# Low halves of the merge-gate weights: a subtraction on VectorE, or an adding transfer onto a negated high half

## The chip, the core and the metric

One core of a Trainium2 chip runs the whole kernel. The metric is device time in microseconds from one launch, the median of several executions. TensorE multiplies, VectorE and ScalarE work elementwise, GpSimd and SyncE here only issue transfers, and sixteen DMA engines carry them.

## What is computed

The reference is a trunk of two layers on 512 tokens of width 1024 (float32). In each layer the normalized input is multiplied by a wide matrix `w_in`; three mixers (sliding-window attention with sinks, gated linear attention, latent attention) work on its parts; and three gates of 1024 channels each weigh their projected outputs:

```python
(qa, ka, va, ga, qb, kb, vb, ab, gb, cq, ckv, kr, gc, mg) = split_cols(h @ w_in)
...
m = jax.nn.sigmoid(mg).reshape(B, S, N_BRANCH, D_MODEL)
y = m[:, :, 0] * za + m[:, :, 1] * zb + m[:, :, 2] * zc
return x + y @ w_out
```

The columns `mg` of `w_in`, 3072 of them, are the merge-gate weights that the change is about.

## The kernel before

**Pieces.** All weights lie in memory as 77 pieces for each layer, 128 partitions by 1024 float32 (512 KB), in the order of their use. `pieces[n]` with n = 77 x layer + p is loaded into `raw`, which has three slots. Every product is made of three matmuls in a reduced-width float type: with a weight split into a high half and a low half, and the input split likewise, it is high x high, high x low and low x high. The halves of a piece lie in `w_hi` and `w_lo`, which have three slots each (`HL = RAW = 3`), n modulo 3. Most pieces hold 128 output columns for a depth of 1024, so they take 8 x 3 = 24 matmuls of 128x128 by 512.

**Who does what to a piece n.**
- SyncE (line 563) waits until the subtraction of piece n - 3 is done (`lo_split`), then issues the load of piece n (line 564). The same queue issues, between these loads, 12 of every 16 transfers that place turned tiles of attention scores (`place_blocks`, line 495), 0.6 us each, so a load waits its turn behind them.
- ScalarE (`split_hi`, line 903) waits for the load and until TensorE has finished piece n - 3, then copies `raw` to `w_hi` with a cast (line 909). It also computes the tanh of each gate (line 1055), the exponentials of the attention scores (lines 1117 and 1129), and issues the other 4 of each 16 transfers.
- VectorE (`split_lo`, line 1208) waits for that copy and subtracts: `w_lo = raw - w_hi` (line 1215). It also empties the accumulation banks (line 1545), makes the silu gates (line 1419), divides and transposes the scores (lines 1485, 1498, 1514) and gates the branches' outputs (line 1230).
- TensorE (`project`, line 577) waits for the subtraction of piece p at its first quarter (line 583) and then issues its matmuls (line 657).
- GpSimd has no work.

**The order.** Each engine walks the same hand-written list, `SCHEDULE`, made by `make_schedule`: quarters of pieces, with named steps between them ("score_a", "divide_a", "turn_a", "send", "value_c", "gate_c" and so on). An engine acts on the names that concern it, strictly in this order. At the second quarter of piece p VectorE splits piece p + 2; at the last quarter ScalarE splits piece p + 3, then does the tanh of piece p, then the steps that follow. So what comes late on an engine makes everything behind it in the list late on that engine.

**The merge-gate pieces** are 22 to 29, 38 to 45 and 57 to 64 of each layer (`PM = [22, 38, 57]`, eight from each), 48 in all. During the first run the linear attention's output is normalized and turned; in the second the sliding-window scores are exponentiated, divided, turned and used (lines 1117, 1485, 1514, 735, 1230); ahead of and in the third run it is the latent attention's scores (lines 868, 1129, 1498, 892). A turned tile leaves VectorE's transposes, is placed by 16 transfers, and is read by the value matmuls (lines 735, 892), which write a bank that VectorE's gate (line 1230) empties.

Of the kernel before, what the change touches and what calls it, by code (L numbers as in the profile page):

```python
# [19 lines left out]
ALU = mybir.AluOpType  # L20
ACT = mybir.ActivationFunctionType
AX_X = mybir.AxisListType.X

DEPTH, D, S, CHUNK, P = 2, 1024, 512, 64, 128
# [20 lines left out]
PM = [22, 38, 57]  # L45
PO = [30, 49, 65]
PUKV, PUQ = 46, 47
PW = 69
PIECES = 77
RAW = HL = 3  # L50
# [33 lines left out]
def emptied_by(r):  # L84

    by_scalar = by_act(r + 1) > by_act(r)
    return not by_scalar, by_scalar


def signals_before(p):  # L90

    return sum(max(outputs_of(q), 1) for q in range(p))
# [212 lines left out]
def build_hybrid_trunk(nc, x_t, pieces, params, alpha, tables, consts, final_g, out, k_rope_dram):  # L305
    with ExitStack() as ctx:
# [3 lines left out]
        def sig(name, per_layer, before=0):  # L310
            return Signal(ctx, nc, name, per_layer, before)
# [5 lines left out]
        raw = sb("raw", [P, RAW, 1024])  # L317
        w_hi = sb("w_hi", [P, HL, 1024], F32R)
        w_lo = sb("w_lo", [P, HL, 1024], F32R)
# [99 lines left out]
        head_hi, head_lo = sig("head_hi", 0), sig("head_lo", 0)  # L419
        eps_set, ones_set = sig("eps_set", 0), sig("ones_set", 0)  # L420
        lat_sq_hi, lat_sq_lo = sig("lat_sq_hi", 2), sig("lat_sq_lo", 2)
        hi_split, lo_split = sig("hi_split", PIECES), sig("lo_split", PIECES)
        proj_done = sig("proj_done", signals_before(PIECES), HL + 1)
        proj_free = sig("proj_free", by_dve(first_output(PIECES)), KT)
        ring_act = sig("ring_act", by_act(first_output(PIECES)))
# [62 lines left out]
        block = ctx.enter_context(nc.Block())  # L488
# [10 lines left out]
        def _(sp):  # L499
            for j in range(KT):  # L500
                sp.dma_start(xt[:, j, :], x_t[:, j, :]).then_inc(x_loaded[j].sem, 16)
                if j == 2:
                    for n in range(2, 4):
                        p, cols = HEADS[n]
# [9 lines left out]
            for n in range(RAW + 1, DEPTH * PIECES):  # L514
                layer, p = divmod(n - RAW, PIECES)
                if p in (PQA[1] + 3, PQA[3] + 3):

                    pair = (PQA[1] + 3, PQA[3] + 3).index(p)
                    sp.wait_ge(rope_out.sem, rope_out.at(layer, 6 + 2 * pair))
                    for hh in range(GROUP):  # L520
                        for half in range(2):
                            sp.dma_start(q_a[64 * pair + 32 * half:64 * pair + 32 * half + 32, hh, :],
                                         work[32 * hh:32 * hh + 32, 4 + half, :]).then_inc(q_placed.sem, 16)
                elif p == PUKV + 3:

                    sp.wait_ge(k_rope_saved.sem, k_rope_saved.at(layer, 16))
                    sp.wait_ge(read_done.sem, read_done.at(layer, 4))
                    for a in range(GROUP):
                        sp.dma_start(k_r[32 * a:32 * a + 32, :], k_rope_dram).then_inc(k_rope_placed.sem, 16)
                elif p == PUQ + 4:  # L530

                    sp.wait_ge(rope_out.sem, rope_out.at(layer, 10))
                    for g, half, a in ((g, half, a) for g in range(2) for half in range(2) for a in range(GROUP)):
                        sp.dma_start(q_r[32 * a + 16 * half:32 * a + 16 * half + 16, g, :],
                                     work[64 * g + 16 * a:64 * g + 16 * a + 16, 2 * half, :]).then_inc(q_rope_placed.sem, 16)
                if p == PM[0] + 3:

                    sp.wait_ge(head_blocks.sem, head_blocks.at(layer, 4))
                    sp.wait_ge(read_done.sem, read_done.at(layer, 4))
                    for n_part in range(SP_PARTS):  # L540
                        place_blocks(sp, 0, n_part, head_placed)
                for group in SENDS.get(p, ()):

                    sp.wait_ge(blocks_set.sem, blocks_set.at(layer, 4 * group + 4))
                    if group < 2:
                        sp.wait_ge(y_pre_set.sem, y_pre_set.at(layer, B_HEADS))
                    elif group > 2:
                        sp.wait_ge(value_done.sem, value_done.at(layer, TT + group - 3))
                    for n_part in range(SP_PARTS):
                        place_blocks(sp, group, n_part, turned_placed)  # L550
                if layer == DEPTH - 1 and PW <= p < PW + 4:

                    m = p - PW
                    sp.wait_ge(x_turned.sem, KT)
                    sp.wait_ge(value_done.sem, value_done.at(layer, TT + n_sets))
                    for b in range(4):
                        sp.dma_start(x_rows[32 * m:32 * m + 32, :, 256 * b:256 * b + 256],
                                     bank_a[32 * b:32 * b + 32, 1024 * m:1024 * m + 1024].rearrange("p (t d) -> p t d", t=TT)
                                     ).then_inc(rows_placed.sem, 16)
                if layer == DEPTH - 1 and p == PW + 4:  # L560
                    sp.wait_ge(merge_lo.sem, merge_lo.at(layer, KT))
                    sp.dma_start(gain, final_g).then_inc(gain_loaded.sem, 16)
                sp.wait_ge(lo_split.sem, n - RAW + 1)
                sp.dma_start(raw[:, n % RAW, :], pieces[n]).then_inc(raw_loaded[n % RAW].sem, 16)
            for t in range(TT):
                sp.wait_ge(scaled_dve.sem, t + 1)
# [9 lines left out]
        def _(pe):  # L576
            def project(layer, quarter):

                p, part = divmod(quarter, 4)
                slot = (layer * PIECES + p) % HL  # L580
                whi, wlo = w_hi[:, slot, :], w_lo[:, slot, :]
                if part == 0:
                    pe.wait_ge(lo_split.sem, lo_split.at(layer, p + 1))
                natural = p in PN1 or p in PN2
                n_out = outputs_of(p)

# [76 lines left out]
            def last_rows():  # L663

                layer, banks = DEPTH - 1, [*(r[:, :] for r in ring), aux[:, :]]

                def row_tile(p, k, t, bank):

                    slot, ts = (layer * PIECES + p) % HL, slice(t * P, (t + 1) * P)
                    cols = slice(k % 2 * HALF, k % 2 * HALF + HALF)  # L670
                    pe.matmul(bank, act_hi[:, k, ts], w_hi[:, slot, cols], start=k == 0, stop=False)  # L671
                    pe.matmul(bank, act_lo[:, k, ts], w_hi[:, slot, cols], start=False, stop=False)  # L672
                    return pe.matmul(bank, act_hi[:, k, ts], w_lo[:, slot, cols], start=False, stop=k == KT - 1)  # L673

                for n in range(4):
                    pe.wait_ge(lo_split.sem, lo_split.at(layer, PW + n + 1))
                    for k in (2 * n, 2 * n + 1):
                        pe.wait_ge(merge_lo.sem, merge_lo.at(layer, k + 1))
                        for t in range(TT):
                            mm = row_tile(PW + n, k, t, nat[t])  # L680
                    mm.then_inc(proj_done.sem, 1)
                pe.wait_ge(proj_free.sem, proj_free.at(layer, by_dve(first_output(PW))))
                pe.wait_ge(o_read.sem, o_read.at(layer, 2 * TT))
                for n in range(2):
                    pe.wait_ge(lo_split.sem, lo_split.at(layer, PW + 4 + n + 1))
                    for k in (2 * n, 2 * n + 1):
                        for t in range(TT):
                            mm = row_tile(PW + 4 + n, k, t, banks[t])
                    mm.then_inc(proj_done.sem, 1)
                for t in range(TT):  # L690
                    for n in range(2, 4):
                        if t == 0:
                            pe.wait_ge(lo_split.sem, lo_split.at(layer, PW + 4 + n + 1))
                        for k in (2 * n, 2 * n + 1):
                            mm = row_tile(PW + 4 + n, k, t, banks[t])
                    mm.then_inc(rows_done.sem, 1)
# [52 lines left out]
            for layer in range(DEPTH):  # L749
                u = 0  # L750
                for name, i in SCHEDULE:
# [82 lines left out]
                    elif name == "score_a":  # L834

                        ready, n = (head_nat, 4) if i == 0 else (exp_done, 4)
# [65 lines left out]
        def _(act):  # L902
            def split_hi(layer, p):

                n = layer * PIECES + p
                act.wait_ge(raw_loaded[n % RAW].sem, 16 * (n // RAW + 1))

                act.wait_ge(proj_done.sem, proj_done.at(layer, signals_before(p - HL + 1) if p >= HL else p - HL + 1))
                nc.scalar.activation(w_hi[:, n % HL, :], raw[:, n % RAW, :], ACT.Copy).then_inc(hi_split.sem, 1)  # L909

            def rms_of(layer, u, place, dst, n, tmp):
# [266 lines left out]
            act.dma_start(out[TT - 1, :, 0:HALF], out_first[:, TT - 1, :]).then_inc(out_sent[1].sem, 16)  # L1178


        @block.vector
        def _(dve):
            def add_square(layer, n):
# [24 lines left out]
            def split_lo(layer, p):  # L1208

                if p >= PIECES:  # L1210
                    layer, p = layer + 1, p - PIECES
                if layer < DEPTH:
                    dve.wait_ge(hi_split.sem, hi_split.at(layer, p + 1))
                    n = layer * PIECES + p
                    nc.vector.tensor_tensor(w_lo[:, n % HL, :], raw[:, n % RAW, :], w_hi[:, n % HL, :].bitcast(F32),  # L1215
                                            ALU.subtract).then_inc(lo_split.sem, 1)
# [555 lines left out]
```

## Time and profile before

| what | us |
|---|---|
| median of three executions (931.48 to 931.8) | 931.62 |
| span of the profiled execution, first to last instruction | 929.7 |
| TensorE busy | 922.0 |
| VectorE busy | 601.2 |
| ScalarE busy | 387.2 |
| GpSimd busy | 0.2 |

The time of the profiled execution is given by its span; the median of the timed ones is 1.9 us longer. A row of a timeline gives the start, the length, engine, line, operation, output and inputs, and in brackets how long the engine had been idle before and what ended that. ACT is ScalarE, DVE VectorE, PE TensorE, SPq and ACTq the transfers that SyncE and ScalarE issue. Matmuls overlap: a row of 0.39 us is followed by the next 0.23 us after its start.

### The profile page before, as it was taken

What the parts mean: (1) busy time and instruction counts of PE and PEld (TensorE: products, weight loads), DVE (VectorE), ACT (ScalarE), POOL (GpSimd) and SP (SyncE); (2) the same over time, 40 slices, a digit from 0 to 9 for tenths busy, and PEclk for the clock granted to TensorE, in tenths of its full rate; (3) what the DMA queues carried; (4) which work ended last, traced back from release to release, by engine and by line L of the source; (5) the groups of instructions that cost most, each with busy time, mean ns of one, the idle gap of its engine ahead of it and who ended that gap; (6) DMA issues with size and microseconds to landing.
All of it is one profiled execution on the core that took longest, in us unless ns stands there. A gap on an engine that the chain in (4) does not pass through costs nothing.

```text
span 929.7 us, 13082 instructions
## 1 busy us (share of the span) xinstructions
PE 922.0 (99%) x5108; PEld 755.8 (81%) x5108; DVE 601.2 (65%) x982; ACT 387.2 (42%) x724; POOL 0.2 (0%) x4
## 2 busy tenths in 40 slices
PE   9999999999999999999999999999999999999997
PEld 7988888888888777888889888888888887778886
DVE  7856467448757877575457664674477568876834
ACT  7453344324543454432444333442264425562324
POOL 0000000000000000000000000000000000000000
PEclk9999999999999999999999999999999999999999
DMA  7324324322434255422232333253234433454542
GB/s 292 136 70 147 114 69 136 113 91 80 140 122 140 85 151 150 145 92 90 91 113 91 95 108 106 68 163 109 91 92 143 140 114 109 122 156 136 146 127 90
DMA packets 43789, 110.98 MB, mean 119 GB/s; under 512 B 8592, under 2 KB 11408, under 8 KB 43600
## 3 DMA queue, kind: packets, MB, share of 16 engines
q1 hardware_dynamic: 39664, 104.82, 35.8%
q10 hardware_dynamic: 4064, 5.33, 2.2%
q8 instruction: 40, 0.66, 0.3%
q14 instruction: 21, 0.17, 0.1%
HBM read 85.41 MB, written 2.23 MB: 94 GB/s over the span
## 4 chain that ended last, share of the span: by engine, by line
PE 86%; DVE 5%; ACT 3%; SPq 2%; issue 1%; DMA 1%; ACTq 1%; DVEq 0%
PE ring L657 65%; PE nat L657 9%; PE nat L868 3%; PE aux L892 2%; SPq L495 1%; DVE w_lo L1215 1%; ACT work L1117 1%; PE nat L672 1%; PE nat L671 1%; PE nat L673 1%; DVE work L1514 1%; DMA raw<-pieces 1%; ACT w_hi L909 1%; PE ring L672 1%; PE ring L671 1%
## 5 line engine op out<-in xcount | busy, mean ns | idle before, releaser
L657 PE MATMUL ring<-act_hi,w_hi 128*128 128x512 f32 x784 | 308.7, 394 | 0.0
L657 PE MATMUL ring<-act_lo,w_hi 128*128 128x512 f32 x784 | 305.5, 390 | 0.0
L657 PE MATMUL ring<-act_hi,w_lo 128*128 128x512 f32 x784 | 305.2, 389 | 0.0
L909 ACT ACTIVATE w_hi<-raw 128x1024 fp32r<-128x1024 f32 x152 | 161.7, 1064 | 340.5 <-PE ring L657 275.5
L1215 DVE TENSOR_TENSOR w_lo<-raw,w_hi 128x1024 fp32r<-128x1024 f32 x152 | 184.6, 1216 | 82.7 <-ACT w_hi L909 82.3
L657 PEld LDWEIGHTS ring<-act_hi,w_hi 128*128 128x128 f32 x784 | 147.1, 188 | 38.2 <-issue 8.4
L657 PEld LDWEIGHTS ring<-act_hi,w_lo 128*128 128x128 f32 x784 | 147.2, 188 | 31.1
L657 PEld LDWEIGHTS ring<-act_lo,w_hi 128*128 128x128 f32 x784 | 147.2, 188 | 29.7
L1545 DVE SCALAR_TENSOR_TENSOR gates<-ring,rstd 128x512 f32<-128x512 f32 x72 | 49.3, 685 | 77.0 <-PE ring L657 76.8
L657 PE MATMUL ring<-y_hi,w_hi 128*128 128x512 f32 x192 | 74.9, 390 | 0.0
L657 PE MATMUL ring<-y_hi,w_lo 128*128 128x512 f32 x192 | 74.7, 389 | 0.0
L657 PE MATMUL ring<-y_lo,w_hi 128*128 128x512 f32 x192 | 74.7, 389 | 0.0
L1055 ACT ACTIVATE gates<-gates 128x512 f32<-128x512 f32 x72 | 45.1, 626 | 18.9 <-DVE gates L1545 18.9
L657 PE MATMUL nat<-w_hi,act_hi 128*128 128x512 f32 (+1 forms) x128 | 48.1, 376 | 0.3 <-DVE w_lo L1215 0.3
L657 PE MATMUL nat<-w_lo,act_hi 128*128 128x512 f32 (+1 forms) x128 | 47.8, 374 | 0.0
L657 PE MATMUL nat<-w_hi,act_lo 128*128 128x512 f32 (+1 forms) x128 | 47.8, 374 | 0.0
L1129 ACT ACTIVATE work<-nat,neg_top 128x256 f32<-128x256 f32 (+3 forms) x48 | 24.7, 530 | 43.9 <-DVE neg_top L1472 43.9
L657 PEld LDWEIGHTS ring<-y_hi,w_hi 128*128 128x128 f32 x192 | 36.0, 188 | 8.1 <-issue 0.7
L657 PEld LDWEIGHTS ring<-y_hi,w_lo 128*128 128x128 f32 x192 | 36.0, 188 | 7.5
L657 PEld LDWEIGHTS ring<-y_lo,w_hi 128*128 128x128 f32 x192 | 36.1, 188 | 7.4
L1595 DVE SCALAR_TENSOR_TENSOR gates<-gates,ring 128x512 f32<-128x512 f32 x32 | 21.9, 685 | 9.0 <-PE ring L657 8.9
L657 PEld LDWEIGHTS nat<-w_hi,act_hi 128*128 128x128 f32 x128 | 24.1, 188 | 3.9 <-DVE w_lo L1215 0.8
(227 smaller groups left out, 995.6 us busy)
## 6 DMA issues: line engine op xcount, KB each, us to landing
raw<-pieces SPq DMA_DIRECT2D x152, 512.0 KB, 3.5
bank_g<-work SPq DMA_DIRECT2D x120, 64.0 KB, 2.0
lat<-work SPq DMA_DIRECT2D x72, 64.0 KB, 2.0
bank_g<-work ACTq DMA_DIRECT2D x40, 64.0 KB, 2.2
xt<-x_t SPq DMA_DIRECT2D x8, 256.0 KB, 4.9
bank_a<-work SPq DMA_DIRECT2D x32, 64.0 KB, 2.0
bank_g<-bank_a SPq DMA_DIRECT2D x16, 128.0 KB, 3.9
out<-gates SPq DMA_DIRECT2D x7, 256.0 KB, 2.1
```

The lines of the kernel that those rows point to most:

```text
L495: engine.dma_start(dst[32 * j:32 * j + 32, S * i:S * i + S], work[32 * i:32 * i + 32, 3 + j, :]).then_inc(placed.sem, 16)
L657: mm = pe.matmul(dst, stationary, moving, start=start and i == 0, stop=stop and i == 2)
L671: pe.matmul(bank, act_hi[:, k, ts], w_hi[:, slot, cols], start=k == 0, stop=False)
L672: pe.matmul(bank, act_lo[:, k, ts], w_hi[:, slot, cols], start=False, stop=False)
L868: mm = pe.matmul(nat[a][:, col:col + n], q, k, start=part == 0, stop=part == 2)
L892: mm = pe.matmul(o_t[r * 64:r * 64 + 64, place, :].rearrange("p (i n) -> p i n", i=4), v_c[:, b, h * C_V:(h + 1) * C_V], turned_c[2 - i % ...
L909: nc.scalar.activation(w_hi[:, n % HL, :], raw[:, n % RAW, :], ACT.Copy).then_inc(hi_split.sem, 1)
L1055: nc.scalar.activation(gates[:, j if j >= 4 else 8 + j, :], gates[:, j, :], ACT.Tanh).then_inc(gate_tanh.sem, 1)
L1129: one = nc.scalar.activation(prob[a][:, keys], nat[a][:, keys], ACT.Exp, scale=C_SCALE, bias=neg_top[:, i % 2, 4 * n + a:4 * n + a + 1], a ...
L1215: nc.vector.tensor_tensor(w_lo[:, n % HL, :], raw[:, n % RAW, :], w_hi[:, n % HL, :].bitcast(F32), ALU.subtract).then_inc(lo_split.sem, 1)
L1545: nc.vector.scalar_tensor_tensor(gates[:, j, :], res, 0.5, rstd[:, :], ALU.mult, ALU.mult).then_inc(proj_free.sem, 1)
L1595: nc.vector.scalar_tensor_tensor(merged[:, j, :] if b == 0 else tile, tile, 1.0, z, ALU.add, ALU.mult).then_inc(proj_free.sem, 1)
```

## The change

For the 48 merge-gate pieces ScalarE writes two tiles from `raw`: first minus the high half into `w_lo`, then the high half into `w_hi`. GpSimd waits for the first, and issues a transfer that reads the piece from memory once more and adds it onto `w_lo`, which then holds the low half. VectorE's subtraction of these pieces is gone. TensorE waits for the landing and for the copy to `w_hi`; there is one semaphore for landings in each slot. SyncE frees a slot of `raw` when both of ScalarE's tiles are written. All other pieces stay as they are, with the counts of `lo_split` taken over them alone.

```diff
+LO_BY_DMA = {p for first in PM for p in range(first, first + 8)}
+
+def lo_by_dve(n):
+    return sum(m % PIECES not in LO_BY_DMA for m in range(n))
+
+def lo_by_dma(n, slot=None):
+    return sum(m % PIECES in LO_BY_DMA and slot in (None, m % HL) for m in range(n))
...
-                sp.wait_ge(lo_split.sem, n - RAW + 1)
+                if p in LO_BY_DMA:
+                    sp.wait_ge(neg_set.sem, lo_by_dma(n - RAW + 1))
+                    sp.wait_ge(hi_split.sem, n - RAW + 1)
+                else:
+                    sp.wait_ge(lo_split.sem, lo_by_dve(n - RAW + 1))
                 sp.dma_start(raw[:, n % RAW, :], pieces[n]).then_inc(raw_loaded[n % RAW].sem, 16)
...
-                    pe.wait_ge(lo_split.sem, lo_split.at(layer, p + 1))
+                    n = layer * PIECES + p
+                    if p in LO_BY_DMA:
+                        pe.wait_ge(lo_added[slot].sem, 16 * lo_by_dma(n + 1, slot))
+                        pe.wait_ge(hi_split.sem, hi_split.at(layer, p + 1))
+                    else:
+                        pe.wait_ge(lo_split.sem, lo_by_dve(n + 1))
...
+                if p in LO_BY_DMA:
+                    nc.scalar.activation(w_lo[:, n % HL, :], raw[:, n % RAW, :], ACT.Copy, scale=-1.0).then_inc(neg_set.sem, 1)
                 nc.scalar.activation(w_hi[:, n % HL, :], raw[:, n % RAW, :], ACT.Copy).then_inc(hi_split.sem, 1)
...
+        @block.gpsimd
+        def _(pool):
+            for n in range(DEPTH * PIECES):
+                if n % PIECES in LO_BY_DMA:
+                    pool.wait_ge(neg_set.sem, lo_by_dma(n + 1))
+                    pool.dma_start(w_lo[:, n % HL, :], pieces[n], accum_op=ALU.add).then_inc(lo_added[n % HL].sem, 16)
...
-                if layer < DEPTH:
+                if layer < DEPTH and p not in LO_BY_DMA:
                     dve.wait_ge(hi_split.sem, hi_split.at(layer, p + 1))
```

## Rows read from the trace of the kernel before

**Rows 1.** The page, part 1: busy us, share, instructions.
```profile
PE 922.0 (99%) x5108; PEld 755.8 (81%) x5108; DVE 601.2 (65%) x982; ACT 387.2 (42%) x724; POOL 0.2 (0%) x4
```

**Rows 2.** The chain of waits, whole run: start us, us, what.
```profile
126.84 84.59 PE ring L657 x372
```

**Rows 3.** Waits of TensorE, whole run: us in total, times, longest us.
```profile
PE aux L744 <- DVE merged L1232: 1.2, 1, 1.2
PE aux L735 <- DMA bank_g<-work: 0.4, 2, 0.2
PE nat L657 <- DVE w_lo L1215: 0.3, 1, 0.3
```

**Rows 4.** The page, part 5: copies to w_hi and subtractions to w_lo.
```profile
L909 ACT ACTIVATE w_hi<-raw 128x1024 fp32r<-128x1024 f32 x152 | 161.7, 1064 | 340.5 <-PE ring L657 275.5
L1215 DVE TENSOR_TENSOR w_lo<-raw,w_hi 128x1024 fp32r<-128x1024 f32 x152 | 184.6, 1216 | 82.7 <-ACT w_hi L909 82.3
```

**Rows 5.** Timeline of ScalarE, 224 to 246 us.
```profile
224.57 1.06 ACT L909 ACTIVATE w_hi<-raw 128x1024 fp32r<-128x1024 f32 x1 [2.18 <-PE ring L657]
225.54 0.62 ACT L1055 ACTIVATE gates<-gates 128x512 f32<-128x512 f32 x1
230.15 2.72 ACTq L495 DMA_DIRECT2D bank_g<-work  x4
232.97 0.21 ACT L1112 ACTIVATE sink_exp<-top 128x8 f32<-128x8 f32 x1 [6.81 <-DVE top L1454]
...
238.68 1.14 ACT L909 ACTIVATE w_hi<-raw 128x1024 fp32r<-128x1024 f32 x1
...
243.07 1.06 ACT L909 ACTIVATE w_hi<-raw 128x1024 fp32r<-128x1024 f32 x1 [0.73 <-PE ring L657]
```

**Rows 6.** Timeline of ScalarE, 129 to 131 us: start, us, what [idle before].
```profile
129.92 1.06 ACT L909 ACTIVATE w_hi<-raw 128x1024 fp32r<-128x1024 f32 x1 [0.95 <-PE ring L657]
```

**Rows 7.** Transfers: queue of SyncE, loads of raw, their landing over the run.
```profile
q1 hardware_dynamic: 39664, 104.82, 35.8%
...
raw<-pieces SPq DMA_DIRECT2D x152, 512.0 KB, 3.5
...
DMA to landing us min/median/max: 3.3/3.5/7.2
```

**Rows 8.** Timeline of SyncE's transfers, 237 to 248 us.
```profile
237.68 9.90 SPq L564 DMA_DIRECT2D raw<-pieces  x4
```

**Rows 9.** Timelines of ScalarE and VectorE, 144 to 151 us.
```profile
149.60 1.06 ACT L909 ACTIVATE w_hi<-raw 128x1024 fp32r<-128x1024 f32 x1 [2.07 <-issue]
...
144.48 1.18 DVE L1215 TENSOR_TENSOR w_lo<-raw,w_hi 128x1024 fp32r<-128x1024 f32 x1
145.59 0.68 DVE L1419 SCALAR_TENSOR_TENSOR gates<-gates 128x512 f32<-128x512 f32 x1
```

**Rows 10.** Timeline of VectorE, 226 to 231 us.
```profile
226.19 0.69 DVE L1419 SCALAR_TENSOR_TENSOR gates<-gates 128x512 f32<-128x512 f32 x1 [0.28 <-ACT gates L1055]
...
230.04 1.18 DVE L1215 TENSOR_TENSOR w_lo<-raw,w_hi 128x1024 fp32r<-128x1024 f32 x1
```

**Rows 11.** Timeline of ScalarE, second layer, copy of piece 41.
```profile
697.04 1.15 ACT L909 ACTIVATE w_hi<-raw 128x1024 fp32r<-128x1024 f32 x1
```

**Rows 12.** Timelines of ScalarE, VectorE and TensorE, 343 to 350 us.
```profile
343.40 1.10 ACT L909 ACTIVATE w_hi<-raw 128x1024 fp32r<-128x1024 f32 x1
344.92 0.63 ACT L1055 ACTIVATE gates<-gates 128x512 f32<-128x512 f32 x1 [0.42 <-DVE gates L1545]
...
344.81 1.47 DVE L1419 SCALAR_TENSOR_TENSOR gates<-gates 128x512 f32<-128x512 f32 x2
...
348.06 0.39 PE L657 MATMUL ring<-act_hi,w_lo 128*128 128x512 f32 x1
348.50 0.77 PE L892 MATMUL aux<-bank_g,bank_a 128*64 128x128 f32 x10
```

More of the change, by code:

```diff
@@ L421, in build_hybrid_trunk @@
         lat_sq_hi, lat_sq_lo = sig("lat_sq_hi", 2), sig("lat_sq_lo", 2)
-        hi_split, lo_split = sig("hi_split", PIECES), sig("lo_split", PIECES)
+        hi_split, lo_split = sig("hi_split", PIECES), sig("lo_split", lo_by_dve(PIECES))
+        neg_set, lo_added = sig("neg_set", 0), [sig(f"lo_added{i}", 0) for i in range(HL)]
         proj_done = sig("proj_done", signals_before(PIECES), HL + 1)
@@ L675, in last_rows @@
                 for n in range(4):
-                    pe.wait_ge(lo_split.sem, lo_split.at(layer, PW + n + 1))
+                    pe.wait_ge(lo_split.sem, lo_by_dve(layer * PIECES + PW + n + 1))
                     for k in (2 * n, 2 * n + 1):
@@ L684, in last_rows @@
                 for n in range(2):
-                    pe.wait_ge(lo_split.sem, lo_split.at(layer, PW + 4 + n + 1))
+                    pe.wait_ge(lo_split.sem, lo_by_dve(layer * PIECES + PW + 4 + n + 1))
                     for k in (2 * n, 2 * n + 1):
@@ L692, in last_rows @@
                         if t == 0:
-                            pe.wait_ge(lo_split.sem, lo_split.at(layer, PW + 4 + n + 1))
+                            pe.wait_ge(lo_split.sem, lo_by_dve(layer * PIECES + PW + 4 + n + 1))
                         for k in (2 * n, 2 * n + 1):
```

## Prediction

> **What bounds the kernel now.** I read the page's busy shares first: TensorE is busy for 922.0 of 929.7 us while VectorE works 601.2 us [rows 1]. A busy TensorE need not be a full one, so the next view is the chain of waits: one link is 372 matmuls in 84.59 us [rows 2], which is 0.2274 us for each, with nothing between them. A piece of 24 matmuls so lasts 5.46 us, and in that stretch the vector engines set nothing. The third view, TensorE's own waits, says what could be won: all it ever waited for an instruction of another engine or a transfer is 1.2, 0.4 and 0.3 us [rows 3]. The first and the last of these lie at the start, before any merge piece. What is left to win is some tenths of a us; the question is what the change can lose. The profiled span of 929.7 us stands 1.9 us under the median of 931.62 us, and I add what I find to the median.
>
> **What the change removes.** 48 of the 152 VectorE subtractions of full pieces go, 1.216 us each [rows 4], 58 us of busy time. They are hidden already: TensorE never waited for one except 0.3 us at the start [rows 3]. Removing them is worth nothing by itself. Only where a VectorE chain leads to TensorE does it help: the wait for the turned tiles, 0.4 us in two places [rows 3], has three or four of these subtractions ahead of it. I count it as won: -0.4 us.
>
> **What it adds on ScalarE.** 48 copies with scale -1, each 1.06 us alone [rows 4] and 0.97 us from its start to that of the next instruction [rows 5]. They are put ahead of the copy to the high half, so that copy, the tanh behind it and everything queued behind that starts 0.97 us later. Most of it is hidden: in the steady stretch ScalarE waits for TensorE before each copy [rows 6], as it does for 275.5 us in all [rows 4]. SyncE's wait for a raw slot moves from the subtraction to the copies, so loads start no later than before. TensorE now waits on a landing and on the copy, two waits in place of one.
>
> **What it adds between the copy and TensorE.** A transfer on GpSimd's queue, which is empty now, and which 512 KB go through. Its time from negated copy to landing, A below, no row shows. From below it is a plain load of the same 512 KB: 3.5 us to landing [rows 7]. A gain below that has no source, because the same bytes come from the same place and are added as well. From above I take a read, an add and a write that don't overlap at all, three plain trips or 10.5 us, and one load beside them. A load's share of the sixteen engines follows from its queue: 35.8% of 929.7 us for 104.82 MB [rows 7] is 1.67 us for each 512 KB; so 12.2 us. In between: 3.5 us, plus 1.67 us because the destination is read too, plus 1.67 us for a raw load beside it gives **6.8 us**. I take that, since it lies nearest to the slowest plain load in the trace, 7.2 us [rows 7], which is what such a transfer takes in company. And there is company: SyncE issues four loads back to back just where it hurts most, from 237.68 us on [rows 8].
> The Trainium skill's page "DMA: Bandwidth & Descriptors" (Anatomy of one DMA, SWDGE path) fits a transfer of this queue as 2.0 us plus its bytes at 436 GB/s. By that a plain 512 KB would take 3.2 us, a second read would make it 4.4 us, and the sum below would be +6.8 us in place of +11.6 us. The row of the same size, 3.5 us from another queue, is 0.3 us over the fit, and no row here shows GpSimd's.
>
> **How much time the transfer has.** The negated copy can start when TensorE ends the piece that held the slot, 0.10 us behind it. Two pieces of 5.46 us then cover it. Taking off 0.10, the copy's 1.06, and 0.16 us by which a matmul starts before its predecessor ends, a transfer has 9.6 us. A of 6.8 us is hidden there. It is not hidden where ScalarE comes late:
> - Piece 26: ScalarE reaches its copy only at 149.60 us, behind four transfers that it issues itself [rows 9]. A subtraction of VectorE's that leads to them (144.48 us, 1.1 us to the next start [rows 9]) goes, the negation comes: its end stays at about 149.6 us. Five pieces after the end that released the copy at 129.92 us [rows 6], TensorE wants it at 157.1 us, so 7.5 us. Hidden. Pieces 28 and 29 come late in the same way and have no less.
> - Piece 41, where ScalarE is deep in sixteen exponentials. Now: copy of piece 40 at 224.57, tanh at 225.54 [rows 5], VectorE's silu waits for the tanh until 226.19 and works on to 230.04, where the subtraction of piece 40 stands [rows 10]; ScalarE issues transfers from 230.15 for 2.72 us, starts exponentials at 232.97, and comes to piece 41 at 238.68 [rows 5]. With a negation in front of copy 40 the tanh, the silu, the transfers and the exponentials all move by 0.97. The subtraction that is dropped at 230.04 stands behind the transposes and takes nothing from the transfers ahead of the exponentials. So the negation of piece 41 starts at 239.65 and ends 1.14 later at 240.79. TensorE ends piece 40 just ahead of 243.07, where the copy that waits for this end starts 0.10 behind it [rows 5], at 242.97. The transfer has 2.2 us and needs 6.8: **TensorE stands for 4.6 us.** In the second layer the same copy stands at 697.04 us [rows 11], 458.36 us after the first with the same queue before it: 9.2 us in all.
> - Behind that, TensorE being late gives the next pieces room, and no later piece starts its copies with less than 9.6 us.
>
> **A second loss, without a transfer.** Where the third branch's scores are divided, ScalarE has two merge pieces in a row. The tanh behind the second starts at 344.92 us, after a wait of 0.42 us for VectorE, while the copy before it starts at 343.40 [rows 12]; at 0.97 us for a copy it was free at 344.37. Two negations add 1.94: 346.31, or 1.4 us later than now. The second of VectorE's two silus at 344.81 needs this tanh, then come reciprocals, division and the gate that frees the bank; TensorE starts on it at 348.50, 0.44 us after the matmul before, where 0.23 is the pace [rows 12]. It is already the last thing waited for, so 1.4 us are paid, in two layers 2.8 us.
>
> **Sum.** 9.2 + 2.8 - 0.4 = +11.6 us: 931.6 + 11.6 = **943 us**. At A of 4.5 us it is 4.6 + 2.4 = +7.0 (939); at 9.5 us 14.6 + 2.4, with 2.0 us at piece 26 in each layer, +21 (953).
>
> **Rivals.**
> 1. *The transfer is longer than two pieces last.* Beyond 9.6 us every merge piece pays. The slot turns once in three pieces, so each three pieces cost A - 9.6. At 12.2 us that is 2.6 us, three times in the first run of eight; in the second run piece 41's 10.0 us covers the rest, the third has slack in its middle and pays about twice: 23 us a layer, 46 + 2.4 makes 980 us; at 10.5 us about 960. For it: nothing shows how an adding transfer overlaps with itself. Against: plain loads never took over 7.2 us.
> 2. *It runs at the pace of a plain transfer, without company.* A of 3.5 to 4.4 us leaves 1.3 to 2.2 us at piece 41: 2.6 or 4.4, and 2.4: 937 to 938 us. Against it: the four loads beside it. The fit of the Trainium skill's page "DMA: Bandwidth & Descriptors" would be this case.
> 3. *Not slower.* The place is piece 41: if the landing comes within 2.2 us of the negation, TensorE doesn't stand there. If the silu behind the two copies also doesn't gate the bank, what remains is the 0.4 us won on the turned tiles, and up to 0.2 us at 348.50 in each layer: 930.8 us. From 2.2 us on it is decided against; the fastest load took 3.3 us [rows 7]. Were the low halves after all ready in time otherwise, for instance because ScalarE gets to piece 41 earlier than I read, the time would be 931 to 933 us.
> 4. *The change doesn't do what it says:* if adding transfers held up the other queues, the turned tiles would come late too. Their row of 0.4 us would grow by a load's 1.67 us in two places: 946 us. This lies inside the range and I give it no chance of its own.
>
> **How the numbers follow.** Forecast (A from 4.5 to 9.6 us; its own range 939 to 953) 0.56; rival 1 0.18; rival 2 0.14; rival 3 0.12. Around 0.2%, or 1.9 us, is what a measurement of this kernel can tell from no change. Rival 3 gives 0.04 faster and 0.08 the same, the others are slower: 0.88. The range begins at 936, just under rival 2, leaving out rival 3, and ends at 968, about A of 11 us, leaving out the upper part of rival 1 (0.08): 0.2 outside.
>
> **What would show it.** In the profile after, a wait of TensorE for a landing in w_lo of some 4 to 5 us ahead of piece 41's first matmul, near 243 us, and again in the second layer; none in the first run of merge pieces; 104 subtractions on VectorE and 200 copies on ScalarE; TensorE's first matmul on the value bank after 348 us about 1.4 us later against the matmul ahead of it. TensorE's wait at the turned tiles is gone. I am wrong if TensorE waits in every third merge piece (rival 1), if the landing comes 3 to 4 us after the negation (rival 2), or if TensorE shows no wait for GpSimd's transfers at all (rival 3).

## The result and the profile after

The changed kernel takes 964.63 us (four executions, 963.95 to 968.53) beside 931.71 us for the kernel before (four, 931.48 to 931.87): a ratio of 1.0361 [1.0349, 1.0373], **33 us slower**. The forecast was 943 us, so the direction was right and the size was not: 11.6 us were foreseen. The profiled execution took 968.53 us with a span of 966.6 us, 36.9 us over the span before; its times are accounted for against that span. It is the longest of the four and has the lowest mean granted clock (0.984, the others 0.987 to 0.991), so the clock's part of the account below is larger than in the median execution.

First the page after: part 1; of part 3 GpSimd's queue (packets, MB, share of the sixteen DMA engines); of part 5 VectorE's subtraction and ScalarE's negated copy; of part 6 the transfers (the last number is the median us to landing).

```profile
PE 932.7 (96%) x5108; PEld 762.2 (79%) x5108; DVE 547.9 (57%) x934; ACT 430.5 (45%) x772; POOL 42.7 (4%) x52
...
q0 software_dynamic: 6912, 25.17, 15.0%
...
L1248 DVE TENSOR_TENSOR w_lo<-raw,w_hi 128x1024 fp32r<-128x1024 f32 x104 | 126.7, 1219 | 64.5 <-ACT w_hi L934 64.4
...
L933 ACT ACTIVATE w_lo<-raw 128x1024 fp32r<-128x1024 f32 x48 | 51.6, 1075 | 61.0 <-PE ring L680 43.3
...
raw<-pieces SPq DMA_DIRECT2D x152, 512.0 KB, 3.9
w_lo<-pieces POOLq DMA_DIRECT2D x48, 512.0 KB, 7.0
...
bank_g<-work ACTq DMA_DIRECT2D x40, 64.0 KB, 4.4
```

The work has moved as the diff says: 48 subtractions gone, 48 copies of 1.075 us added, VectorE 53 us less busy than in [rows 1 and 4]. TensorE's busy time has grown by 10.7 us with the same 5108 matmuls, so it not only waited more, it also worked more slowly somewhere. And transfers that were not changed take longer: tiles that ScalarE issues land after 4.4 us, where the page of before has 2.2:

```profile
bank_g<-work ACTq DMA_DIRECT2D x40, 64.0 KB, 2.2
```

What TensorE waited for comes next (line waited for: us in total, times, longest), to be set against [rows 3].

```profile
PE ring L680 <- DMA w_lo<-pieces: 16.1, 5, 6.3
PE aux L758 <- DMA bank_g<-work: 6.2, 2, 3.2
PE aux L915 <- DVE y_pre L1263: 3.2, 2, 1.8
...
PE ring L735 <- ACT act_hi L968: 0.8, 1, 0.8
PE nat L680 <- DVE w_lo L1248: 0.6, 1, 0.6
```

Where these stand shows TensorE's timeline (start, length, instruction, idle time before it). L680 is the piece's matmul, L758 the matmul on the turned tiles, L915 the one on the value bank.

```profile
170.85 0.50 PE L680 MATMUL ring<-act_hi,w_hi 128*128 128x512 f32 x1 [2.35 <-DMA w_lo<-pieces]
...
171.43 0.63 PE L680 MATMUL ring<-act_hi,w_lo 128*128 128x512 f32 x1
171.85 0.63 PE L680 MATMUL ring<-act_hi,w_hi 128*128 128x512 f32 x1
...
247.44 0.39 PE L680 MATMUL ring<-act_hi,w_lo 128*128 128x512 f32 x1
254.17 0.79 PE L680 MATMUL ring<-act_hi,w_hi 128*128 128x512 f32 x1 [6.35 <-DMA w_lo<-pieces]
...
278.65 1.09 PE L758 MATMUL aux<-bank_g,bank_a 128*64 128x128 f32 x16 [2.96 <-DMA bank_g<-work]
...
367.33 1.86 PE L915 MATMUL aux<-bank_g,bank_a 128*64 128x128 f32 x30 [1.83 <-DVE y_pre L1263]
...
648.08 0.50 PE L680 MATMUL ring<-act_hi,w_hi 128*128 128x512 f32 x1 [2.45 <-DMA w_lo<-pieces]
...
729.83 0.80 PE L680 MATMUL ring<-act_hi,w_hi 128*128 128x512 f32 x1 [4.75 <-DMA w_lo<-pieces]
...
753.95 1.09 PE L758 MATMUL aux<-bank_g,bank_a 128*64 128x128 f32 x16 [3.21 <-DMA bank_g<-work]
```

Four places in each layer: piece 28 (170.85, 648.08), piece 41 (254.17, 729.83), the turned tiles (278.65, 753.95) and the value bank (367.33, and 1.42 us in the second layer). No other merge piece stands by more than some tenths.

Behind five of these stands TensorE works at the lower clock. The stretches in which it does, in the view of busy time by windows (window and its length; busy us of PE, PEld, DVE, ACT, POOL; granted clock, DMA share, GB/s):

```profile
171.40:174.80 3.40, 3.40 (x9) 2.64 (x8) 0.00 (x0) 0.00 (x0) 0.00 (x0) 0.50 1.04 274
254.20:260.10 5.90, 5.90 (x36) 4.86 (x38) 1.05 (x2) 0.32 (x1) 0.00 (x0) 0.50 1.06 276
649.30:652.60 3.30, 3.30 (x9) 2.51 (x9) 0.00 (x0) 0.00 (x0) 0.00 (x0) 0.50 0.98 323
729.90:734.50 4.60, 4.60 (x24) 3.56 (x26) 0.00 (x0) 0.00 (x0) 0.00 (x0) 0.50 1.07 280
755.10:758.40 3.30, 3.30 (x20) 2.62 (x16) 3.10 (x4) 0.67 (x2) 0.00 (x0) 0.50 0.51 163
```

The granted clock is 0.50, 1.2 in place of 2.4 GHz, for 20.5 us in which TensorE is busy all the time. A matmul starts 0.42 us after the one before it there (171.43 and 171.85), where the pace is 0.23, so at the full clock the same work takes about half. That is some 10.3 us, nearly all of the 10.7 us by which TensorE's busy time has grown.

**The account of the span:** TensorE's idle time (span less busy time) has grown from 7.7 to 33.9 us, that is by 26.2. Of these the landings in `w_lo` are 16.1, the turned tiles 6.2 less the 0.4 that they cost before, the value bank 3.2, and the last two waits above 0.8 and 0.3 more than before. With the 10.7 us of busy time, 10.3 of them the lower clock, that is the whole 36.9 us.

### The profile page after: what moved, and what is told of

Same layout as the page of the kernel before. It is cut to its first block, busy times and chain, and to the rows that moved or that the text cites. A ratio compares the mean times of both kernels' runs of the same rounds, so it can differ in the third digit from the quotient of the medians.

```text
span 966.6 us, 13174 instructions
## 1 busy us (share of the span) xinstructions
PE 932.7 (96%) x5108; PEld 762.2 (79%) x5108; DVE 547.9 (57%) x934; ACT 430.5 (45%) x772; POOL 42.7 (4%) x52
## 4 chain that ended last, share of the span: by engine, by line
PE 75%; DMA 6%; ACT 6%; DVE 6%; SPq 4%; issue 2%; ACTq 1%; DVEq 0%
PE ring L680 54%; PE nat L680 8%; SPq L509 3%; DMA w_lo<-pieces 3%; DMA raw<-pieces 2%; PE nat L891 2%; PE aux L915 2%; ACT w_lo L933 1%; ACT w_hi L934 1%; ACTq L509 1%; ACT work L1154 1%; DVE work L1547 1%; DMA bank_g<-work 1%; ACT work L1142 1%; PE nat L696 1%
## 5 line engine op out<-in xcount | busy, mean ns | idle before, releaser
L680 PE MATMUL ring<-act_hi,w_hi 128*128 128x512 f32 x784 | 312.3, 398 | 16.1 <-DMA w_lo<-pieces 16.1
L680 PE MATMUL ring<-act_hi,w_lo 128*128 128x512 f32 x784 | 307.9, 393 | 0.0
L680 PE MATMUL ring<-act_lo,w_hi 128*128 128x512 f32 x784 | 307.9, 393 | 0.0
L934 ACT ACTIVATE w_hi<-raw 128x1024 fp32r<-128x1024 f32 x152 | 161.2, 1061 | 279.4 <-PE ring L680 226.0
L680 PEld LDWEIGHTS ring<-act_hi,w_hi 128*128 128x128 f32 x784 | 148.7, 190 | 57.3 <-DMA w_lo<-pieces 18.4
L680 PEld LDWEIGHTS ring<-act_hi,w_lo 128*128 128x128 f32 x784 | 148.5, 189 | 31.7
L680 PEld LDWEIGHTS ring<-act_lo,w_hi 128*128 128x128 f32 x784 | 148.9, 190 | 30.0
L1248 DVE TENSOR_TENSOR w_lo<-raw,w_hi 128x1024 fp32r<-128x1024 f32 x104 | 126.7, 1219 | 64.5 <-ACT w_hi L934 64.4
L1212 POOL DMA_DIRECT2D w_lo<-pieces x48 | 42.5, 885 | 834.9 <-ACT w_lo L933 834.9
L933 ACT ACTIVATE w_lo<-raw 128x1024 fp32r<-128x1024 f32 x48 | 51.6, 1075 | 61.0 <-PE ring L680 43.3
L680 PE MATMUL ring<-y_hi,w_hi 128*128 128x512 f32 x192 | 74.9, 390 | 0.0
L680 PE MATMUL ring<-y_hi,w_lo 128*128 128x512 f32 x192 | 74.7, 389 | 0.0
L680 PE MATMUL ring<-y_lo,w_hi 128*128 128x512 f32 x192 | 74.7, 389 | 0.0
L680 PE MATMUL nat<-w_hi,act_hi 128*128 128x512 f32 (+1 forms) x128 | 48.1, 376 | 0.6 <-DVE w_lo L1248 0.6
L680 PE MATMUL nat<-w_lo,act_hi 128*128 128x512 f32 (+1 forms) x128 | 47.8, 374 | 0.0
L680 PE MATMUL nat<-w_hi,act_lo 128*128 128x512 f32 (+1 forms) x128 | 47.8, 374 | 0.0
L680 PEld LDWEIGHTS ring<-y_hi,w_hi 128*128 128x128 f32 x192 | 36.0, 188 | 8.1 <-issue 0.7
L680 PEld LDWEIGHTS ring<-y_hi,w_lo 128*128 128x128 f32 x192 | 36.0, 188 | 7.5
L680 PEld LDWEIGHTS ring<-y_lo,w_hi 128*128 128x128 f32 x192 | 36.0, 188 | 7.4
```

The lines of the kernel that those rows point to most:

```text
L680: mm = pe.matmul(dst, stationary, moving, start=start and i == 0, stop=stop and i == 2)
L933: nc.scalar.activation(w_lo[:, n % HL, :], raw[:, n % RAW, :], ACT.Copy, scale=-1.0).then_inc(neg_set.sem, 1)
L1212: pool.dma_start(w_lo[:, n % HL, :], pieces[n], accum_op=ALU.add).then_inc(lo_added[n % HL].sem, 16)
```

## Experiments

Three theories stood. **M:** the landings come late at a few pieces, and the clock falls behind the stands. **T:** the adding transfers as traffic slow the other queues, and with them the turned tiles. **S:** ScalarE's 48 further copies alone delay what hangs on ScalarE. In the diffs `GATES` are the 48 merge pieces.

**Copies alone** (on the kernel before: ScalarE writes the negated half, VectorE subtracts over it as ever)

```diff
+                if p in GATES:
+                    nc.scalar.activation(w_lo[:, n % HL, :], raw[:, n % RAW, :], ACT.Copy, scale=-1.0).then_inc(neg_set.sem, 1)
                 nc.scalar.activation(w_hi[:, n % HL, :], raw[:, n % RAW, :], ACT.Copy).then_inc(hi_split.sem, 1)
...
+                    if p in GATES:
+                        dve.wait_ge(neg_set.sem, sum(m % PIECES in GATES for m in range(n + 1)))
```

> The kernel before, with ScalarE's 48 negated copies added and no adding transfer: VectorE still subtracts and overwrites them. If the loss is ScalarE's (theory S), the time rises by 10 us or more. If it is the late landings (theory M) or the traffic of the adding transfers (theory T), only the value bank behind the two copies in a row comes late, as I predicted: 1.4 us in each layer, about 934 to 935 us, no clock of TensorE lost, turned tiles waited for as before (0.2 us each).

Measured: 939.86 us, ratio 1.0086 [1.0071, 1.0101]. TensorE's waits:

```profile
PE aux L739 <- DMA bank_g<-work: 3.3, 2, 1.7
PE aux L896 <- DVE y_pre L1238: 2.8, 2, 1.4
```

The value bank comes 1.4 us late in each layer, as forecast to the tenth. The turned tiles already wait up to 1.7 us with no further transfer in the kernel, and the expectation had missed that: ScalarE, which computes the exponentials ahead of the tiles and issues a quarter of their transfers, comes to both later (its second four issues start at 256.19 us, before at 253.52). So S is a real part, 7.8 us here; but VectorE still subtracts in this kernel, and behind two copies, so these are not the changed kernel's shares. The clock stays up until the last 2 to 3 us, as it does before.

**Traffic alone** (on the kernel before: GpSimd copies the 48 pieces from memory to memory, and nobody waits for it)

```diff
+        @block.gpsimd
+        def _(pool):
+            for n in range(DEPTH * PIECES):
+                if n % PIECES in GATES:
...
+                    pool.wait_ge(hi_split.sem, n + 1)
+                    pool.dma_start(spare[n % 3], pieces[n]).then_inc(beside[n % 3].sem, 16)
```

> The kernel before, with one more transfer of 512 KB by GpSimd for each merge piece, from memory to a spare place in memory, waited for by nobody but GpSimd itself. It holds the sixteen engines about half as long as an adding one. Theory T: the transfers that place turned tiles come late, TensorE's wait for them grows from 0.2 us to 1 us or more in each layer, ScalarE's four issues near 230 us take over 3.3 us instead of 2.7, and the time rises by 3 us or more. Theories M and S: the wait and the issues stay, time within 1 us of before.

Measured: 942.08 us, ratio 1.011 [1.0093, 1.0127]. TensorE's waits:

```profile
PE aux L739 <- DMA bank_g<-work: 7.0, 2, 3.7
PE aux L896 <- DVE y_pre L1247: 1.8, 2, 1.3
```

Transfers on which nothing hangs make the turned tiles wait 3.5 us in each layer. T is real, and it was the rival of the prediction that got no chance of its own. Of the expected signs one failed where it was placed: ScalarE's four issues near 230 us take 2.71 us as before; the next four, at 253.70 us, take 3.88 and before 2.46. The value bank waits 1.8 us here with no copies added, so ScalarE's two copies in a row are not the only thing that can make it late.

**Without pieces 28 and 41** (on the changed kernel, as all that follow; a piece taken out goes back to VectorE's subtraction)

```diff
-LO_BY_DMA = {p for first in PM for p in range(first, first + 8)}
+LO_BY_DMA = {p for first in PM for p in range(first, first + 8)} - {28, 41}
```

> The changed kernel with pieces 28 and 41 of each layer left to VectorE, the other 44 by adding transfers. Theory M (late landings and the clock that falls behind them): TensorE's waits for landings vanish (16 us), and with them most of the 10.5 us of clock; left are the turned tiles and the value bank: 938 to 944 us. Theory T: the slow transfers make other pieces or the turned tiles late in their place, 950 us or more. Theory S: 955 us or more.

Measured: 945.3 us, ratio 1.0139 [1.0124, 1.0155]. TensorE's waits:

```profile
PE aux L758 <- DMA bank_g<-work: 4.7, 2, 2.7
PE aux L915 <- DVE y_pre L1263: 3.0, 2, 1.6
PE ring L680 <- DMA w_lo<-pieces: 2.8, 4, 1.5
```

Two of 24 pieces of a layer carry 19 of the 33 us: the four stands and most of the stretches at the lower clock go with them (one is left, after the turned tiles of the second layer). It ended just over the expected range, as neighbours of the two pieces now wait up to 1.5 us.

**A plain transfer in place of the adding one.** It overwrites `w_lo` with the raw weight, so the subtraction of the merge pieces is left out.

```diff
-                    pool.dma_start(w_lo[:, n % HL, :], pieces[n], accum_op=ALU.add).then_inc(lo_added[n % HL].sem, 16)
+                    pool.dma_start(w_lo[:, n % HL, :], pieces[n]).then_inc(lo_added[n % HL].sem, 16)
```

> The changed kernel with GpSimd's transfer as a plain one: it overwrites the negated copy with the raw weights, so the subtraction is left out for the merge pieces. If adding is what is slow (its packets take 327 ns where plain ones take 159), time to landing falls from 7.0 to about 5.5 us, and the stalls at pieces 28 and 41 shrink by 1.3 to 2.5 us each: 950 to 957 us. If GpSimd's path as such is slow, the time to landing stays near 7 us and the time near 964 us. Were the traffic all of it, 940 us or less.

Measured: 942.1 us, ratio 1.0112 [1.0097, 1.0128]. GpSimd's queue on its page:

```profile
q0 software_dynamic: 6912, 25.17, 9.1%
```

TensorE's waits:

```profile
PE ring L680 <- DMA w_lo<-pieces: 3.9, 2, 2.0
PE aux L915 <- DVE y_pre L1263: 2.8, 2, 1.4
PE aux L758 <- DMA bank_g<-work: 1.2, 2, 0.9
```

The landings of GpSimd's line (L1212):

```profile
DMA to landing us min/median/max: 3.6/4.2/7.5
```

With the copies, the waits and the traffic of a plain transfer kept, 22 of the 33 us are gone, far more than I expected: they go with the addition within the transfer. For the same packets and bytes the queue has the sixteen engines busy for 9.1% of 939.6 us in place of 15.0% of 966.6 us, 1.7 times less. The Trainium skill's page "Collectives: The Full Stack" (Part 3, the bandwidth ceiling) says of ReduceScatter, a collective that adds within its transfers, that the add costs no cycles of its own but needs two source reads, and measures a factor of 1.93 there. The 1.7 here points the same way, and no run here separates the second read from the add.

**Piece 41 alone**

```diff
-LO_BY_DMA = {p for first in PM for p in range(first, first + 8)}
+LO_BY_DMA = {41}
```

> Only piece 41 of each layer by an adding transfer, all other merge pieces as before. ScalarE then reaches it as early as before (238.7 us), the negation ends near 239.8 and TensorE wants it at 242.9: 3.1 us. If a landing takes 7 us whatever is beside it, TensorE stands 3.9 us in each layer; if company made the 7 us, the landing takes 5.5 us and TensorE stands 2.4 us. With or without a fall of the clock behind it (1.7 us each in the changed kernel): 936 to 943 us. If the other adding transfers and not this piece were the cause, the time is that of before.

Measured: 944.41 us, ratio 1.0137 [1.0123, 1.015]. The one large new wait of TensorE:

```profile
PE ring L680 <- DMA w_lo<-pieces: 8.5, 2, 4.4
```

Busy time by windows, behind the stand of each layer:

```profile
248.50:252.00 3.50, 3.50 (x18) 2.56 (x18) 0.00 (x0) 0.00 (x0) 0.00 (x0) 0.50 0.01 2
714.00:717.00 3.00, 3.00 (x23) 2.35 (x23) 0.02 (x1) 0.00 (x0) 0.00 (x0) 0.50 0.02 5
```

Here the account can be seen by itself. The stands are 4.4 and 4.1 us, close to the prediction's 4.6 each and over the 3.9 expected of this run, whose range ended at 943 us. The granted clock is 0.50 from 246.23 us for 6.83 us and from 713.85 us for 3.41 us; what of it lies behind the stands (the first ends at 247.89, the second before 713.85), 5.2 and 3.4 us, costs about half, 4.3 us. 8.5 + 4.3 is 12.8; the median is 12.7 us slower, and the span of the profiled execution, whose waits these are, 13.5 (943.2 us). The DMA share in these stretches is 0.01 and 0.02, so it is the clock and no transfer that makes TensorE slow there.

**The first run of merge pieces alone** (22 to 29)

```diff
-LO_BY_DMA = {p for first in PM for p in range(first, first + 8)}
+LO_BY_DMA = set(range(22, 30))
```

> Only the first run, pieces 22 to 29. Theory: the landing of piece 28 is waited for 2.5 us in each layer and 1.7 us of clock goes behind it, since VectorE's wait for the tiles of the linear attention grows (3.9 us before, 5.7 in the changed kernel) and makes ScalarE late at piece 28: 940 us. If piece 28 is late only because of extra work on ScalarE, VectorE's wait stays at 3.9 us.

Measured: 937.48 us, ratio 1.006 [1.0046, 1.0074]: landings 2.5 us in all (1.93 and 0.58), where 2.5 in each layer were expected, and one stretch at the lower clock, 3.41 us from 170.89. VectorE's wait for the tiles does grow, to 5.7 us at most.

**The second run alone** (38 to 45)

```diff
-LO_BY_DMA = {p for first in PM for p in range(first, first + 8)}
+LO_BY_DMA = set(range(38, 46))
```

> Only the second run, pieces 38 to 45. If the losses of the runs add up, this one has what the first (8.4 us) and the third (about 3 us at the value bank) leave of 33 us: about 953 us, with 5 to 6.5 us of waiting at piece 41, 2 to 3 us at the turned tiles and the clock behind both, in each layer. If the second run only paid for lateness that the first one left, it is under 945 us.

Measured: 957.19 us, ratio 1.027 [1.0256, 1.0284]: the largest part. TensorE's waits:

```profile
PE ring L680 <- DMA w_lo<-pieces: 10.8, 2, 5.7
PE aux L758 <- DMA bank_g<-work: 7.9, 2, 4.0
```

The runs add up: 5.7 us for the first, 25.5 for the second, and for the third, which was not run by itself, the 2.8 us of the value bank in "copies alone"; 34.0 beside 32.9 us. It was 4 us slower than expected, as TensorE waits 3.9 us for the turned tiles in each layer and not 2 to 3.

**Pieces 42 and 43 alone**, in the search for a version that gains

```diff
-LO_BY_DMA = {p for first in PM for p in range(first, first + 8)}
+LO_BY_DMA = {42, 43}
```

> Only pieces 42 and 43: their two subtractions stand ahead of the transposes whose tiles TensorE waits for (0.37 us over the pace in each layer), and both have over 9 us from negation to first matmul. If the subtractions gate the tiles, the wait vanishes: 0.7 us faster than before, 931.0 us. If ScalarE's copies or the transfers beside the tiles cost as much, it is the same or up to 5 us slower.

Measured: 932.29 us, ratio 1.0008 [0.9999, 1.0017], no change. The 0.4 us at the turned tiles [rows 3] is gone, as the prediction's step said, and TensorE waits 0.2 us for a landing instead. These landings are the longest of all. In each layer the second adding transfer is issued 2.8 or 2.9 us behind the first, which is still under way, and raw loads and tiles run beside both; the first land after 9.1 and 8.8 us, the second after 11.9 and 10.3:

```profile
DMA to landing us min/median/max: 8.8/9.7/11.9
```

**Without the four pieces whose transfers run beside the tiles** (25, 26, 44, 45)

```diff
-LO_BY_DMA = {p for first in PM for p in range(first, first + 8)}
+LO_BY_DMA = {p for first in PM for p in range(first, first + 8)} - {25, 26, 44, 45}
```

> The changed kernel with pieces 25, 26, 44 and 45 of each layer left to VectorE: these are the ones whose adding transfers run beside the 16 transfers that place turned tiles (near 146 to 154 us and 265 to 276 us). If the adding transfers hold up the tiles, VectorE's wait for the linear attention's tiles is back to 3.9 us and piece 28 is in time, and TensorE's wait at the later tiles falls from 3.1 us to under 1 us in each layer; left are piece 41 with its clock (16 us) and the value bank (3 us): 948 to 952 us. If the tiles are late because TensorE's own stand at piece 41 moved everything, the second wait stays at 3 us and the time is over 955 us.

Measured: 950.37 us, ratio 1.0201 [1.0184, 1.0218]. TensorE's waits:

```profile
PE ring L680 <- DMA w_lo<-pieces: 10.6, 2, 5.5
PE aux L915 <- DVE y_pre L1263: 2.8, 2, 1.4
```

VectorE's waits for the linear attention's tiles, before, in the changed kernel and here:

```profile
DVE bank_a L1430 <- DMA bank_g<-work: 6.5, 2, 3.9
...
DVE bank_a L1463 <- DMA bank_g<-work: 10.9, 2, 5.7
...
DVE bank_a L1463 <- DMA bank_g<-work: 4.4, 2, 2.5
```

TensorE's wait for the turned tiles is gone, and so is the one at piece 28, which still has its adding transfer: both came from the neighbours. (Their copies on ScalarE are gone here too; but with every copy kept and a plain transfer the tiles cost 1.2 us and not 6.2, so most of it is the adding transfers.) Piece 41 stays, with the clock behind it, and the value bank.

**Seven pieces out** (25, 26, 28, 41, 44, 45, 58)

```diff
-LO_BY_DMA = {p for first in PM for p in range(first, first + 8)}
+LO_BY_DMA = {p for first in PM for p in range(first, first + 8)} - {25, 26, 28, 41, 44, 45, 58}
```

> The changed kernel with seven pieces of each layer left to VectorE: 25, 26, 44 and 45 (beside the tiles), 28 and 41 (ScalarE late) and 58 (two copies in a row ahead of the value bank). If these seven carry the loss, the other 34 adding transfers of the two layers are hidden: 932 to 935 us, TensorE at full clock. If the loss is spread over all adding transfers, 34 of 48 keep two thirds of it: over 945 us.

Measured: 936.6 us, ratio 1.0052 [1.0036, 1.0068], a little over the expected range. In the profiled execution, the shortest of six (934.22 us), landings cost 1.9 us in two places and the value bank 1.1, and the clock does not fall before the last 3 us of the kernel; the others go up to 940.13 us, and what they lose beyond that was not profiled. The other 17 pieces of each layer go through the adding transfer almost for nothing; seven carry 28 of the 33 us. No version was measurably faster than the kernel before: there were only tenths to win.

## Why the prediction was right and wrong

**Right: the bound and two of the four places.** Removing 58 us of VectorE work won no time. The 0.4 us at the turned tiles are gone only where the adding transfers beside them are left out or few, in the kernels without 25, 26, 44 and 45 and with 42 and 43 alone, and no measured time shows it. "Its time from negated copy to landing", taken as 6.8 us, is 7.06 us at piece 41 (copy's end 247.11, TensorE's start 254.17) and in the kernel with piece 41 alone GpSimd's two transfers land 6.9 and 7.2 us after their issue. Its three terms (3.5 us, 1.67 for the second read, 1.67 for a load beside it) hold one by one in size: in the packets of the traces the plain transfer issued at 226.0 us has no other beside it and lands after 3.7 us, the adding one issued at 619.5 us has 64 KB beside it and lands after 5.4, and the two of piece 41 alone have about one load beside them. A usual merge piece needs less than its 9.6 us, so it doesn't stand: rival 1, in which every piece pays, didn't happen. Rival 2 took a landing of 3.5 to 4.4 us; that is the plain transfer (4.2 us, and 942.1 us for its kernel), while the adding one takes 7.0. For rival 3 the landing would have had to come within 2.2 us.

The fit of the Trainium skill's page "DMA: Bandwidth & Descriptors" (Anatomy of one DMA, SWDGE path) gave an estimate of 3.2 us for the plain transfer and 4.4 us with a second read; the runs show 3.7 and 5.4 us for these two least disturbed transfers, and medians of 4.2 and 7.0 us (5.4 to 11.1) among the others. So the estimate was 0.5 and 1.0 us low, and the larger part of what it lacks for the adding one is what shares the engines with it.

**Right: the value bank.** "1.4 us are paid, in two layers 2.8 us": 1.83 and 1.42 us in the changed kernel, 1.4 each in "copies alone", where nothing else is in the way.

**Wrong first: the sum ends where the stand ends.** In it a stand of TensorE costs its own length. Five of the eight stands cost more: the granted clock falls to 0.50 in or behind the stand and stays there while the next matmuls run. These are 10.3 us in the profiled execution, the largest part of what was missed there, and shown by the kernel with piece 41 alone, where stands and clock make up the whole loss. The Trainium skill's page "TensorE: Matmul & The Clock Gate" (HAM oscillation) says that a TensorE waiting for a transfer can start the next work at the lower clock, and prices it as the time at that clock times one half; the trace agrees (half of 20.5 us beside 10.7 us more of busy time), and the prediction should have weighed it.

**Wrong second: the turned tiles.** They were "counted as won: -0.4 us", and their coming late, rival 4, had "no chance of its own". They cost 5.8 us more in place of 0.4 less. Two causes can do it, each by itself: ScalarE later (3.3 us in "copies alone") and traffic (7.0 us in "traffic alone"), both with VectorE's subtractions kept, so these are no shares of the 6.2. In the changed kernel it is the adding transfers for the most part: 1.2 us are left with plain ones, and nothing without those of pieces 25, 26, 44 and 45. The price in rival 4, a load's 1.67 us in each place, was too small as well: 48 adding transfers take 15.0% of 966.6 us, 3.0 us of the engines for each, and several of them run beside the tiles.

**Wrong third: piece 28.** It was to "come late in the same way and have no less" than piece 26's 7.5 us. The chain of waits after shows it (start, length, what):

```profile
154.13 8.15 DMA raw<-pieces
...
162.30 1.07 ACT w_lo L933
...
163.71 7.09 DMA w_lo<-pieces
...
170.85 29.34 PE ring L680 x121
```

The negation starts at 162.30 and ends at 163.37. TensorE's last matmul of piece 27 starts at 168.11, so the transfer has 5 us and takes over 7. The last to come ahead of the negation is the raw load, with 8.15 us over the 7.2 us at most before [rows 7], but it is the smaller part. ScalarE's timeline before (first row, with the copy of piece 28 right behind it, at 159.02) and after:

```profile
158.48 0.63 ACT L1106 ACTIVATE y_hi<-bank_a 128x512 fp32r<-128x512 f32 x1 [1.55 <-DVE bank_a L1430]
...
160.74 0.64 ACT L1131 ACTIVATE y_hi<-bank_a 128x512 fp32r<-128x512 f32 x1 [0.42 <-DVE bank_a L1463]
162.30 1.06 ACT L933 ACTIVATE w_lo<-raw 128x1024 fp32r<-128x1024 f32 x1 [0.93 <-DMA raw<-pieces]
```

ScalarE waits 0.93 us for the load. It was 2.26 us late already, behind VectorE, which waits for the linear attention's tiles 5.69 us here and 2.60 us before in this layer. The step took the times of loads and tiles from a trace without adding transfers. That the neighbours do this is shown by the kernel without 25, 26, 44 and 45, where piece 28 is in time.

**Right in kind, off in size: piece 41.** Forecast 4.6 us, measured 6.35 and 4.75. The working "all move by 0.97" holds up to ScalarE's four transfers; then ScalarE's timeline after shows what [rows 5] doesn't:

```profile
235.95 4.20 ACTq L509 DMA_DIRECT2D bank_g<-work  x4
...
245.96 1.15 ACT L933 ACTIVATE w_lo<-raw 128x1024 fp32r<-128x1024 f32 x1
```

Issuing them takes 4.20 us where it took 2.72. The negation starts 7.28 us later than the copy before (238.68), while TensorE ends piece 40 only 4.86 us later (247.83 against 242.97). The difference of 2.42 us is the forecast 0.97 and these 1.48. In the second layer the four issues take 2.72 us as before, and TensorE stands 4.75 us, the forecast's 4.6. That it also stands 4.4 and 4.1 us with piece 41 alone is in part luck: no copy ahead is delayed there, so the transfer has 3.1 us and not 2.2, and it takes 7.5 and 7.3 us from the copy's end and not 6.8.

**The numbers.** Forecast 9.2 at piece 41, measured 11.1; nothing at piece 28, measured 4.8; 2.8 at the value bank, measured 3.2; -0.4 at the tiles, measured +5.8; nothing for the clock, measured 10.3. The upper end of the range, 968, was set by a rival that did not happen; that it holds the result is not to its credit.

## What to carry to other kernels

Work that is hidden already is worth nothing when it is removed, and handing it to a transfer costs whatever the transfer does to its neighbours: ask for each added transfer which loads and tiles share its stretch, and price them as longer than in the trace of before. A stand of a TensorE that is full can cost more than its length; look at the granted clock behind it, and add about half of the stretch at the lower clock. Where few pieces are late, send just these another way: seven of 24 carried 28 of 33 us here.

## What was not expected of the hardware

- An adding transfer of 512 KB from memory takes 5.4 to 11.1 us to land, a plain one by the same queue 3.6 to 7.5, with 1.7 times the engines' busy time. GpSimd's instruction itself is 0.875 us, against 0.530 for the plain one.
- Other queues feel it: transfers of 64 KB issued by ScalarE land after 4.4 us and not 2.2. The four near piece 41 take 4.20 us to issue in the first layer and not 2.72 (2.72 in the second layer and with the plain transfer, 3.06 with the second run alone). What in the queues does this is open: it was not tried with transfers that add from on-chip memory, or with another split of the tiles' transfers.
- The clock falls behind short stands, but not behind all. TensorE stood 2.35 and 2.45 us at piece 28 and the clock fell both times; behind the stand of 2.96 us at the tiles of the first layer it didn't, behind that of 3.21 us in the second it did. In the kernel with a plain transfer it fell behind one of two stands of 1.97 us. What decides is open.
